# State space stage of a decoder kernel: the sums of both directions in one bank, step sizes on C times B, one mixing matrix on unweighted tokens

## The reference

```python
def ssd_chunked(x, dt, A, Bm, Cm):
    xdt = (x * dt[..., None]).reshape(b, c, CHUNK, G, r, P)
    adt = jnp.moveaxis((dt * A).reshape(b, c, CHUNK, G, r), 2, -1)
    a_cs = jnp.cumsum(adt, axis=-1)
    CB = jnp.einsum('bclgn,bcsgn->bcgls', Cc, Bc)
    Wd = CB[:, :, :, None] * segsum_exp(adt)          # exp of the sum of a between s and l, l >= s
    y_diag = jnp.einsum('bcgrls,bcsgrp->bclgrp', Wd, xdt)
    states = jnp.einsum('bcsgn,bcgrs,bcsgrp->bcgrpn', Bc, decay_states, xdt)
    ...                                               # scan over the chunks, y_off from the states
    return (y_diag + y_off).reshape(b, l, H, P)

y = y_fwd + y_bwd + d_skip[:, None] * xs              # y_bwd: the same on flipped tokens, with its own dt and A
y = y * silu(z); y = y * rsqrt(mean(y * y in a group) + EPS) * norm_g
```

## Time and profile before

| | |
|---|---|
| median of 3 runs | 2548.49 us (2546.55 to 2549.35) |
| the profiled execution, its own time | 2552.66 us |
| span in its profile | 2550.4 us |
| TensorE busy | 2322.0 us, 91% |
| VectorE busy | 1484.2 us, 58% |
| ScalarE busy | 1003.9 us, 39% |
| GpSimd busy | 536.6 us, 21% |
| mean granted clock of TensorE | 0.94 |

### The profile page before, as it was taken

One profiled execution on the slowest core, in us unless ns is written; L12 is line 12 of the kernel. 1 busy time (PEld: TensorE's weight loads), 2 busy tenths in 40 slices (PEclk: granted clock), 3 DMA queues, 4 the chain that ended last, 5 costly groups with the idle time before them and its releaser, 6 DMA issues.

```text
span 2550.4 us, 33159 instructions
## 1 busy us (share of the span) xinstructions
PE 2322.0 (91%) x12293; PEld 1949.7 (76%) x12293; DVE 1484.2 (58%) x2225; ACT 1003.9 (39%) x1606; POOL 536.6 (21%) x613
## 2 busy tenths in 40 slices
PE   7999989999999799989999999999988997969994
PEld 6887767888888587868888878997768995757772
DVE  3555456888888754363333435567746555466664
ACT  3254523444444432353223332555333334155552
POOL 1000004555556300000000000392234440011001
PEclk8999998999999899888999999999988998979997
DMA  5310221111211433122233240322000006159995
GB/s 184 99 59 9 68 83 50 50 49 58 71 53 50 164 101 99 50 83 80 86 99 99 83 133 25 125 84 75 30 13 1 1 1 228 71 198 382 416 409 185
DMA packets 166444, 267.99 MB, mean 105 GB/s; under 512 B 9050, under 2 KB 140458, under 8 KB 156458
## 3 DMA queue, kind: packets, MB, share of 16 engines
q1 hardware_dynamic: 161849, 249.98, 28.1%
q0 software_dynamic: 4464, 16.25, 1.7%
HBM read 237.38 MB, written 28.84 MB: 104 GB/s over the span
## 4 chain that ended last, share of the span: by engine, by line
PE 68%; DVE 13%; DVEq 6%; ACT 5%; issue 4%; POOL 1%; DMA 1%; POOLq 1%; ACTq 0%; SPq 0%
PE ps L168 16%; PE ps L170 16%; PE ps L169 16%; PE ps L3410 3%; DVE arena L1631 2%; PE ps L2841 1%; PE ps L596 1%; PE ps L993 1%; ACT pair L354 1%; PE ps L2856 1%; PE ps L1015 1%; DVE arena L1667 1%; DVEq L1657 1%; DVEq L1630 1%; DVE ring_rounded L1618 1%
## 5 line engine op out<-in xcount | busy, mean ns | idle before, releaser
L170 PE MATMUL ps<-pair,pair 128*128 128x512 f32 (+1 forms) x2248 | 824.3, 367 | 0.0
L168 PE MATMUL ps<-pair,pair 128*128 128x512 f32 (+1 forms) x1992 | 750.1, 377 | 39.9 <-DVE pair L383 14.2
L169 PE MATMUL ps<-pair,pair 128*128 128x512 f32 (+1 forms) x1992 | 750.3, 377 | 0.0
L170 PEld LDWEIGHTS ps<-pair,pair 128*128 128x128 f32 x2248 | 434.3, 193 | 71.0
L168 PEld LDWEIGHTS ps<-pair,pair 128*128 128x128 f32 x1992 | 385.4, 193 | 104.5 <-issue 40.8
L169 PEld LDWEIGHTS ps<-pair,pair 128*128 128x128 f32 x1992 | 386.7, 194 | 71.0 <-issue 6.9
L354 ACT ACTIVATE pair<-ring 128x2048 fp32r<-128x2048 f32 x102 | 194.8, 1909 | 292.7 <-PE ps L170 287.0
L360 DVE TENSOR_TENSOR pair<-ring,pair 128x2048 fp32r<-128x2048 f32 x95 | 218.8, 2303 | 143.5 <-ACT pair L354 143.4
L1751 POOL TENSOR_TENSOR arena<-arena 128x256 f32<-128x256 f32 x128 | 91.4, 747 | 502.9 <-ACT arena L1528 502.9
L1743 POOL TENSOR_TENSOR pair<-arena,pair 128x512 fp32r<-128x512 f32 x128 | 156.3, 1250 | 58.2 <-PE ps L1399 58.2
L2117 POOL MEMSET arena<- 128x1 f32 x32 | 1.0, 99 | 661.4 <-DVEq L157 661.2
(11 more groups left out here) (502 smaller groups left out, 3910.1 us busy)
## 6 DMA issues: line engine op xcount, KB each, us to landing
ring<-in_w_in SPq DMA_DIRECT2D x54, 1024.0 KB, 6.5
arena<-in_w_exp_down SPq DMA_DIRECT2D x23, 1024.0 KB, 10.7
ring<-in_w_up SPq DMA_DIRECT2D x16, 1024.0 KB, 5.5
ring<-in_w_down SPq DMA_DIRECT2D x16, 1024.0 KB, 5.1
ring<-in_w_exp_gate SPq DMA_DIRECT2D x16, 1024.0 KB, 8.8
ring<-in_w_exp_up SPq DMA_DIRECT2D x16, 1024.0 KB, 10.8
expert_results<-arena SPq DMA_DIRECT2D x23, 512.0 KB, 11.2
ring<-in_w_in SPq DMA_DIRECT2D x16, 512.0 KB, 5.7
```

The lines of the kernel that those rows point to most:

```text
L168: nc.tensor.matmul(out, lhs[1], rhs[0], start=start, stop=False)
L169: nc.tensor.matmul(out, lhs[0], rhs[1], start=False, stop=False)
L170: return nc.tensor.matmul(out, lhs[0], rhs[0], start=False, stop=stop)
```

## The change

The sums of both directions of a chunk go into one PSUM bank: above the diagonal the backward mask gives nothing, below it the forward one, and so one exponential serves both. `sums`, `decay` and `mixers` then run once for a chunk, not for each n, and banks 4 and 6 alternate over chunks. The step sizes dt move from the tokens to C times B: ScalarE scales the forward `cb` by the forward dt of each head into a new buffer `stepped` (`forward_steps`, four copies of 128x128), VectorE adds the backward `cb` times the backward dt in place (four scalar_tensor_tensor of 128x128), drains, and multiplies with `ex` in one 128x512 product. `M` has one matrix for each head and chunk; it is applied to the unweighted `xt`. GpSimd's two `weighted` calls with dt go. The waits move with it.

```diff
-            xw = core.take(4, NT, GW)
+            xw = core.take(2, NT, GW)
+            stepped = core.take(NT, GH * P)
-            M = xw[:, 2:4].rearrange("p a c n -> p (a c n)").rearrange("p (a n) -> p a n", a=4)
+            M = xw.rearrange("p a c n -> p (a c n)").rearrange("p (a n) -> p a n", a=4)
...
+            def step_of(g, d, c, r):
+                return dt[:, d, c, columns(g * GH + r, 1)]
...
-                def sums(g, n):
-                    pe.wait_ge(am_ready, g * 8 + (n + 1))
-                    if n == 0:
+                def sums(g, c):
+                    if c == 0:
                         pe.wait_ge(z_stored, g * 4 + 4)
-                    if n == 1:
-                        after(pe, y_stored, g * 2)
-                    after(pe, ex_ready, g * 8 + (n - 1))
-                    mask = (strict.hi, strict.lo)[n % 2][:, 0, :]
-                    nc.tensor.matmul(ps[:, SUMS[n % 2], :], mask, am[n % 2].lo[:, 0, :], start=True, stop=False)
-                    nc.tensor.matmul(ps[:, SUMS[n % 2], :], mask, am[n % 2].hi[:, 0, :], start=False, stop=True)\
-                        .then_inc(diff_ready, 1)
+                    if c >= 2:
+                        pe.wait_ge(ex_ready, g * 4 + (c - 1))
+                    for d, mask in enumerate((strict.hi, strict.lo)):
+                        pe.wait_ge(am_ready, g * 8 + (2 * c + d + 1))
+                        nc.tensor.matmul(ps[:, SUMS[c % 2], :], mask[:, 0, :], am[d].lo[:, 0, :], start=d == 0, stop=False)
+                        mm = nc.tensor.matmul(ps[:, SUMS[c % 2], :], mask[:, 0, :], am[d].hi[:, 0, :], start=False, stop=d == 1)
+                    mm.then_inc(diff_ready, 1)
...
                     sums(g, 0)
-                    sums(g, 1)
+                    after(pe, y_stored, g * 2)
...
-                            pe.wait_ge(xw_ready, g * 4 + 4)
...
                         for r in range(GH):
-                            for d in range(2):
-                                mm = nc.tensor.matmul(ps[:, 7, r * 64:(r + 1) * 64],
-                                                      M[:, (2 * c + d) % 4, r * P:(r + 1) * P],
-                                                      xw[:, d, c, r * 64:(r + 1) * 64], start=d == 0, stop=d == 1)
+                            mm = nc.tensor.matmul(ps[:, 7, r * 64:(r + 1) * 64], M[:, c, r * P:(r + 1) * P],
+                                                  xt[:, c, r * 64:(r + 1) * 64], start=True, stop=True)
...
+                def decay(g, c):
+                    act.wait_ge(diff_ready, g * 4 + (c + 1))
+                    if c >= 2:
+                        act.wait_ge(m_ready, g * 4 + (c - 1))
+                    act.activation(ex[:, c % 2, :], ps[:, SUMS[c % 2], :], ACT.Exp).then_inc(ex_ready, 1)
+
+                def forward_steps(g, c):
+                    act.wait_ge(cb_read, g + 1)
+                    for r in range(GH):
+                        ins = act.activation(stepped[:, c, r * P:(r + 1) * P], cb[:, 0, c, :], ACT.Copy,
+                                             scale=step_of(g, 0, c, r))
+                    ins.then_inc(forward_stepped, 1)
...
                         if c + 1 < NT:
-                            decay(g, 2 * c + 2)
-                            decay(g, 2 * c + 3)
+                            forward_steps(g, c + 1)
+                            decay(g, c + 1)
...
                     silu_z(g + 1)
+                    forward_steps(g + 1, 0)
                     store_y(g)
                     decay(g + 1, 0)
-                    decay(g + 1, 1)
...
-                    dve.tensor_tensor(heads(M[:, n % 4, :]), heads(ex[:, n % 2, :]),
-                                      cb[:, d, c, :].unsqueeze(1).to_broadcast([P, GH, P]), ALU.mult)\
-                        .then_inc(m_ready, 1)
+                def mixers(g, c):
+                    dve.wait_ge(forward_stepped, g * 4 + (c + 1))
+                    for r in range(GH):
+                        both = stepped[:, c, r * P:(r + 1) * P]
+                        dve.scalar_tensor_tensor(out=both, in0=cb[:, 1, c, :], scalar=step_of(g, 1, c, r), in1=both,
+                                                 op0=ALU.mult, op1=ALU.add)
+                    dve.drain()
+                    dve.wait_ge(ex_ready, g * 4 + (c + 1))
+                    dve.tensor_tensor(M[:, c, :], ex[:, c % 2, :], stepped[:, c, :], ALU.mult).then_inc(m_ready, 1)
...
                 def steps(g, n):
                     c, d = n // 2, n % 2
-                    if n >= 2:
-                        gp.wait_ge(diff_ready, g * 8 + (n - 1))
+                    if c and d == 0:
+                        gp.wait_ge(diff_ready, g * 4 + c)
...
                     gp.wait_ge(tok_ready, g * 3 + 2)
-                    weighted(g, 2, wst)
-                    weighted(g, 3, wst)
-                    for n in range(2):
-                        steps(g, n)
-                    weighted(g, 0, dt)
-                    weighted(g, 1, dt)
-                    for n in range(2, 4):
+                    weighted(g, 0, wst)
+                    weighted(g, 1, wst)
+                    for n in range(4):
                         steps(g, n)
```

More of the change, by code:

```diff
@@ L1300, in stages_ssd @@
             split_before = core.slots
+            forward_stepped = sem("ssd_forward_steps_applied")
             w_hi, w_split = (sem(f"ssd_{n}_then_expert_{later[n]}") for n in ("weights_hi_made", "weights_split"))
@@ L1438, in front @@
                     turn_last()
-                    pe.wait_ge(xw_ready, g * 4 + 2)
+                    pe.wait_ge(xw_ready, g * 2 + 2)
                     pe.wait_ge(tok_ready, g * 3 + 3)
@@ L1445, in front @@
                             mm = nc.tensor.matmul(ps[:, n // 2, (n % 2) * GW:(n % 2 + 1) * GW], Bt[:, c, :],
-                                                  xw[:, 2 + d, c, :], start=True, stop=True)
+                                                  xw[:, d, c, :], start=True, stop=True)
                             n += 1
@@ L1455, in back @@
                         if c + 1 < NT:
-                            sums(g, 2 * c + 2)
-                            sums(g, 2 * c + 3)
+                            sums(g, c + 1)
                         t = slice(c * P, (c + 1) * P)
@@ L1534, in silu_z @@
                                        ACT.Silu).then_inc(z_stored, 1)
-                def decay(g, n):
-                    act.wait_ge(diff_ready, g * 8 + (n + 1))
-                    after(act, m_ready, g * 8 + (n - 1))
-                    act.activation(ex[:, n % 2, :], ps[:, SUMS[n % 2], :], ACT.Exp).then_inc(ex_ready, 1)
+                def decay(g, c):
[9 more added lines that the diff above has]
+                    ins.then_inc(forward_stepped, 1)
                 def square(g, c):
@@ L1584, in first @@
                     weights_hi(1, 1)
+                    forward_steps(0, 0)
                     decay(0, 0)
-                    decay(0, 1)
                 def middle(g, more):
@@ L1660, in states @@
                     dve.drain().then_inc(prev_ready, 1)
[L1662 to L1669 removed]
+                def mixers(g, c):
[7 more added lines that the diff above has]
+                    dve.tensor_tensor(M[:, c, :], ex[:, c % 2, :], stepped[:, c, :], ALU.mult).then_inc(m_ready, 1)
                 def back(g, between):
                     mixers(g, 0)
[L1673 removed]
                     for c in range(NT):
                         if c + 1 < NT:
[L1676 to L1677 removed]
+                            mixers(g, c + 1)
                         else:
```

16 lines of the change are left out of this document (4 added, 12 removed).

## The result

The changed kernel is slower: the median of four runs is 2587.3 us (2584.54 to 2593.99), beside 2548.92 us for the kernel before; the ratio is 1.0166, with an interval of 1.0149 to 1.0183, or some 42 us of 2548.49 (the two medians differ by 38). The forecast of 2571 had the sign and came out 16 to 20 us too low. The median lies inside the range of 2546 to 2590; by the ratio (2548.49 x 1.0166 = 2590.8) the time lies just above its upper end.

What follows compares the result with a forecast made beforehand. A loop of waits through TensorE and VectorE was taken as the bound. Period 60.0 at full clock plus 3.0 slow clock, against 60.13: 20 over seven; last group 2; +22, forecast 2571 us, range 2546 to 2590.

Steps and rivals of the forecast that it cites:

- The turns: VectorE's mixers beside GpSimd: short products alternate with GpSimd's instructions, about 0.95 us each; 4.9 us a chunk instead of 1.93.
- T: Start of a head group's first mixer instruction on VectorE, from which the times of a period are counted.
- F: End of TensorE's next features behind the first y products; forecast 11.5 us after T at full clock, 9.7 before.
- the ruler: Head group used as yardstick in the kernel before: its 59.24 us period ran wholly at 2.4 GHz; mean 60.13.
- The clock behind the first wait: TensorE after waiting for the first mixer: slow clock expected in every group, 2.0 us a period.
- The clock in the second part: TensorE between last features and z products, idle ahead of the transposes: slow clock in part, 1.0 us, bounds 0 and 3.
- TensorE no longer ends the features late: Second part: ScalarE's silus start before the convolution ends, GpSimd starts about 1.6 us sooner, Newton steps gain 0.75 us.
- VectorE's relief: Second part, to the next T: scalings 1.35, weights about 0.3 and Newton steps 0.75 us, sum 2.4 off 28.06.
- The last group: Group with no features to hide behind: two mixers beside GpSimd take T to norm from 21.1 to about 23 us.
- Short products don't queue: Rival at the mixers: 128-wide products slip between GpSimd's instructions; 12 us off, 2537; chance 0.14.
- Clock as before: Rival: TensorE's slow clock costs 0.9 us a period on average, as before; +7.6, about 2556; chance 0.22.
- Slow clock all over: Rival: both slow TensorE stretches in full, 66 us a period, +42, 2590; chance 0.06.

Runs made afterwards that it cites:

- Holding GpSimd back: Changed kernel, with GpSimd's masks of chunk 2 made only once the first mixer product is done: 2565.69 us, ratio 1.0085.
- the kernel with filler: Changed kernel plus sixteen unread 512-wide products on TensorE ahead of its wait for the first mixer: 2578.06 us, ratio 1.0134.
- weights ahead: VectorE's weights for the last features moved before chunk 2's mixers: changed kernel 2577.85 us, ratio 1.0136; kernel before 2551.98 us, 1.0032.
- copies ahead: Changed kernel, with ScalarE making the next chunk's scaled copies before it waits for the features: 2562.67 us, ratio 1.0068.
- taking the short form off VectorE: Changed kernel, copies ahead, ScalarE scaling both directions, VectorE left with one 512-wide addition and one product: 2541.65 us, ratio 0.9990.

## Why the prediction was right in sign and short in size

**The turns.** Right. The first mixer was to be done at T + 4.9 and was at T + 4.5 (677.96), TensorE's wait was to be 4 to 5 us and was 4.15. From F to the second mixer of the ruler 6.6 us were worked out and 6.58 measured (687.65 to 694.23), mixer 3 added 0.6 against 0.65. Holding GpSimd back showed the cause. The Trainium skill's rule (SBUF — State Buffer, "Who interferes with whom") that a VectorE instruction with two SBUF inputs and a GpSimd instruction that reads SBUF exclude each other holds here as it stands: an L1674 takes 0.345 us in the median and 1.127 at most.

**The clock behind the first wait.** Right place, too small a price. F was to be T + 11.5 and 2.0 for the clock; it came at T + 14.2. From the first y products, 0.95 and 5.6 at full clock would end at 684.6; they ended at 687.65, 3.1 later, and the kernel with filler gives the same 3.1 (T + 11.1). The 2.0 was the difference of two periods of the kernel before, whose wait was half as long. There too F came 3.1 us later in the slow period (494.96 less 482.15 is 12.8, against 9.7 in the ruler), and only 2.0 of it reached the next T. So at F this term is short by 1.1 us, less 0.4 for the earlier mixer. How much of that reaches T in the changed kernel is not shown: with the filler, 0.7 of the 3.1 came through to the transposes.

**The clock in the second part.** Wrong place. I put 1.0 us on the way from the last features to the z products. There the clock of the ruler was 1.00 (713.00 to 737.81), as in four more of the seven periods; only in the last two was it 0.93 and 0.90 from the transposes on. In the ruler the second slow stretch came at 702.00, at the head of the last features, behind the wait of 3.33 us. The last features took 7.08 us (702.01 to 709.09) where they took 5.66 at full clock (687.99 to 693.65 in the kernel before), 1.4 more, and this was not hidden from TensorE: the transposes start 3.9 us behind their end in both kernels (693.65 to 697.54, 709.09 to 712.99).

**The step that failed: "TensorE no longer ends the features late".** I let the last features end at F + 16 and from that gave the Newton steps 0.75 us back. But the last features need the weights that VectorE makes behind the mixers of chunk 2, y and the second convolution. My own count of VectorE had them at F + 14.3: the mixer of chunk 2 at F + 6.6, and 7.7 us from there to the weights (680.21 to 687.93 in the kernel before). They came at F + 14.3 (701.96). So the last features could not end before F + 20; TensorE waited 3.33 us for L1626, and with the slow stretch they ended at F + 21.4 (709.09). The silus, the transposes and GpSimd follow.

What that cost came by TensorE, whose z products I had rightly called without slack. I put the z products at F + 25; they came at F + 26.8 (714.45). From the transposes on TensorE waits for nothing until the next T, and it turns y (726.75) 0.5 us after VectorE has done the scalings (726.25). In the kernel before it was the other way round; TensorE waited for the scalings:

```profile
687.99 0.50 PE L168 MATMUL ps<-pair,ring_rounded 128*128 128x512 f32 x1 [0.97 <-DVE ring_rounded L1618]
...
712.54 1.09 PE L1407 MATMUL ps<-arena,ring 128*128 128x128 f32 x8 [1.09 <-DVE ring L1706]
```

From the transposes to the next T it was 26.17 us (697.54 to 723.71), and TensorE alone has 24.8 us of work there. So of the 2.4 us that I gave for VectorE's relief only 1.35 could come off in this stretch, and did. The rest needed transposes that start sooner, and the late features made them late.

The Newton steps show the same lateness, but they did not set the time. GpSimd was to start 1.6 us sooner; in the ruler it started 4.3 us ahead of the norm where it had been 5.2 ahead (699.64 against 704.87 in the kernel before). All four steps then took the turn, and from the norm to the scalings it was 5.71 us, not 5.13: 0.6 lost, 0.75 expected as gained. With TensorE 0.5 us behind, not all of these 1.3 us could have moved T. In the first three periods nothing was lost there and nothing gained: from the norm to the end of the scalings 6.3 us, not 7.6, the relief of the scalings alone.

TensorE's wait of 0.97 us for L1618 at 687.99, shown above, would have told me to look. I passed over it because it was small; from 417 to 800 us it stands in one group only, while in the changed kernel the wait for these weights stands in all six.

**The period.** For the ruler: first part 34.2 + 2.0 predicted, 36.8 measured (673.46 to 710.28); second part 25.6 + 1.0 predicted, 27.5 measured, 1.5 us over in all. Read along TensorE the same 1.5 is: F 0.7 late, the z products 1.8 more, less the 1.0 of clock that was not there. Over the seven, 20 predicted and 29.3 measured.

**The last group.** 2 predicted, 4.0 measured, and 1.4 behind it: the whole group ran at 1.2 GHz. Against that stands the earlier start of the first group, 3.3, which I had not worked out.

**The level.** These terms make the profiled execution 2584.54, where the sum gave 2574.7: 10 us of the miss. The other 7 are how the profiled execution stands to the rest: it lay 4.2 above the median before and lies 2.8 below it after. That is the spread of the runs and no mechanism.

**The rivals.** "Short products don't queue" is refuted. "Clock as before" too. "Slow clock all over" gave 2590, nearest in number, but its mechanism was both slow stretches as I had placed them, and the second was there in the last two periods only. That its number is the nearest is luck.

**What stays open.** What the failed step costs by itself is not isolated: taking the wait away (weights ahead) gained 8 us by the middle values, within the uncertainty, and changed the clock behind it. How the 52 us of the short products divide into turns, ScalarE's copies and clock can't be said in one sum, since the gains overlap: 21 by holding GpSimd back, 25 by copies ahead, 29 by both, 45 by taking the short form off VectorE. Why the move of the weights makes the kernel before slower was not pursued.

## What to carry to other kernels

Count the two-input VectorE instructions that run beside GpSimd, not their length: here four of 128 columns cost 2.8 to 3.1 us there and 1.1 us alone, and one of 512 cost 1.37 there and 0.69 alone. Work cut into short pieces belongs on an engine that GpSimd does not slow (ScalarE's four copies took 1.26 us beside it, at 689.29, and without it, at 698.38), or at a time when GpSimd is silent. When a step gets later, look for every wait behind it in the old trace, above all the small ones (0.97 us here): they are the places where the next engine had almost no slack, and this one grew to 3.33 us. When an engine gets relief, ask which engine comes next: of the 2.4 us expected from VectorE's relief 1.35 could count, as long as TensorE did not start its own part sooner. And compare experiments in groups: gains on one chain don't add, here 0.81% and 0.98% gave 1.15%.

## What the runs showed of the hardware that was not expected

- Not every short product pays. At the head of the ruler group the four start at 673.46, 673.73, 674.35 and 675.40 and last 0.35, 0.70, 1.12 and 1.12 us: those that overlap one of GpSimd's L1750 (1.08 us each, from 674.24 on) take about as long as it does, the second meets a shorter one (L1769, 0.75 us), and the first goes free. So four took 3.06 and, at chunk 2, 2.77 us, not four turns of 0.95.
- The slow clock stretch is not removed by keeping TensorE busy at one place: with sixteen filler products the head ran at 1.00, the clock was low for longer behind the next wait (3.46 us, ahead of the last features), and the transposes behind the wait of 2.46 us went from 1.71 to 2.58 us.
- Four scaled copies of 128x128 on ScalarE with a scale from memory take 1.26 us, the 1.25 that was estimated from other shapes.
